# A fused decoder layer: attention values with the values stationary and the output transposed

## What is computed

```python
hn = rms_norm(x, norm_mix_g[l])
q_a, k_a, v_a, q_m, k_m, v_m, o_m, i_m, f_m = jnp.split(hn @ w_in[l], SPLIT_POINTS, axis=-1)
att = swa_sink_attention(q_a, k_a, v_a, ...)      # 8 heads of 64, 2 key/value heads, window 128, T5 bias, sink
h_m = mlstm_chunkwise(...)                        # 4 heads, normalised, gated
x = x + jnp.concatenate([att, h_m], axis=-1) @ w_out[l]
x = x + hier_moe(rms_norm(x, norm_ffn_g[l]), ...) # 16 experts, top 2 of one group of 4
...
# in the attention
p = jnp.exp(logits - m)
probs = p / (jnp.sum(p, axis=-1, keepdims=True) + jnp.exp(sink_l - m))
out = jnp.einsum('bnkgqs,bnskd->bnqkgd', probs, vb)
```

## Time and profile before

| | |
|---|---|
| median of 3 runs | 928.12 us (925.28 to 929.41) |
| the profiled execution | 928.41 us |
| its span, first to last instruction | 926.6 us |
| mean granted TensorE clock | 0.97 |
| TensorE busy | 868.4 us |
| VectorE busy | 616.1 us |
| ScalarE busy | 563.1 us |
| GpSimd busy | 250.0 us |

### The profile page before, as it was taken

The page is one execution under the profiler, slowest core; times in us unless marked ns, Lnnn a source line. Parts: engine busy times, 40 slices in busy tenths (PEclk is TensorE's granted clock), DMA queues, the critical chain, the costliest instruction groups (busy, mean ns, idle before and its releaser), DMA issues. The chain is left out here.

```text
span 926.6 us, 18029 instructions
## 1 busy us (share of the span) xinstructions
PE 868.4 (94%) x5329; PEld 697.2 (75%) x5330; DVE 616.1 (66%) x1257; ACT 563.1 (61%) x1004; POOL 250.0 (27%) x395
## 2 busy tenths in 40 slices
PE   5899999999999999999973899999999999999994
PEld 4679888898989887788862776776777788677873
DVE  3667666666566677643678766773769599775992
ACT  3473746556473857222241766783879799787991
POOL 4102021010101010000023243553354544445442
PEclk9989999999999998999995899999999999999997
DMA  9810000101010142344473877786698999779963
GB/s 329 250 27 24 24 23 23 45 0 45 0 45 23 47 182 69 137 157 138 159 273 119 316 264 228 257 306 157 228 350 318 322 392 392 269 277 337 393 254 68
DMA packets 57646, 168.41 MB, mean 182 GB/s; under 512 B 12584, under 2 KB 14928, under 8 KB 57616
## 3 DMA queue, kind: packets, MB, share of 16 engines
q1 hardware_dynamic: 50384, 143.13, 41.7%
q0 software_dynamic: 7232, 24.92, 10.4%
HBM read 143.49 MB, written 24.54 MB: 181 GB/s over the span
## 5 line engine op out<-in xcount | busy, mean ns | idle before, releaser
L1034 PE MATMUL bank_j<-w_high,rows_high 128*128 128x512 f32 x512 | 207.6, 405 | 8.0 <-DVE w_low L1637 5.5
L1036 PE MATMUL bank_j<-w_high,rows_low 128*128 128x512 f32 x512 | 201.8, 394 | 0.0
L1035 PE MATMUL bank_j<-w_low,rows_high 128*128 128x512 f32 x512 | 201.7, 394 | 0.0
L597 POOL TENSOR_TENSOR tick<-mhalf 1x1 f32<-1x1 f32 x176 | 89.4, 514 | 200.6 <-DVE lg L2064 73.7
L1034 PEld LDWEIGHTS bank_j<-w_high,rows_high 128*128 128x128 f32 x512 | 97.4, 190 | 39.8 <-issue 12.9
L1952 DVE TENSOR_TENSOR w_low<-w_res,w_high 128x1024 fp32r<-128x1024 f32 x96 | 114.2, 1217 | 7.1 <-ACT w_high L695 7.1
L1036 PEld LDWEIGHTS bank_j<-w_high,rows_low 128*128 128x128 f32 x512 | 97.3, 190 | 21.2
L1035 PEld LDWEIGHTS bank_j<-w_low,rows_high 128*128 128x128 f32 x512 | 97.6, 191 | 18.3
L695 ACT ACTIVATE w_high<-w_res 128x1024 fp32r<-128x1024 f32 x96 | 97.5, 1050 | 0.2 <-PE bank_j L1036 0.2
L1139 PE MATMUL bank_j<-hnT,w_res 128*128 128x128 f32 x512 | 60.3, 276 | 0.0
L543 POOL TENSOR_TENSOR rqk<-ssqk,eps_hd 128x10 f32<-128x10 f32 x8 | 5.8, 728 | 201.1 <-DVE ssqk L1833 201.1
(11 more groups left out here) (367 smaller groups left out, 1832.9 us busy)
## 6 DMA issues: line engine op xcount, KB each, us to landing
w_res<-in_w_gate_dram SPq DMA_DIRECT2D x48, 512.0 KB, 7.4
w_res<-in_w_up_dram SPq DMA_DIRECT2D x48, 512.0 KB, 7.2
bias<-in_w_down_dram SPq DMA_DIRECT2D x32, 512.0 KB, 7.5
slot_b<-in_w_gate_dram SPq DMA_DIRECT2D x16, 512.0 KB, 10.5
PT<-in_w_up_dram SPq DMA_DIRECT2D x16, 512.0 KB, 11.6
gmix<-in_w_down_dram SPq DMA_DIRECT2D x16, 512.0 KB, 6.5
h<-in_w_down_dram SPq DMA_DIRECT2D x16, 512.0 KB, 8.3
hn<-in_x_dram SPq DMA_DIRECT2D x8, 512.0 KB, 3.4
```

The source lines that it names most:

```text
L597: pool.tensor_tensor(tick[:, len(ticks):len(ticks) + 1], mhalf[0:1, 0:1], mhalf[0:1, 0:1], ALU.mult)
L1034: pe.matmul(out_, ah, bh, start=start, stop=False)
L1035: pe.matmul(out_, ah, bl, start=False, stop=False)
L1036: return pe.matmul(out_, al, bh, start=False, stop=stop)
```

## The change

`values` now keeps the values stationary, 64 columns of one key/value head at a time, and streams the transposed probabilities of two heads (256 columns). Its output is transposed: head columns by queries, the key/value head 0 in partitions 0 to 63 and head 1 in 64 to 127 of O0. The reciprocal sums must then be scaled per column. `prob_scales` (VectorE) spreads `arc` over 512 columns of `lg`, `sums_T` (TensorE) transposes them in four blocks into T0, `head_copy` (ScalarE) copies O0 into `mix`, and `attention` (VectorE) multiplies this in place with T0. The first 512 columns of a stored row tile are thus already transposed: `mix_T` transposes only the other half, and `mix_high` and `mix_low` read the first half from `hn` in SBUF. The rows of `w_out` are loaded in the matching order, and `load_mix` has stricter waits, since `hn` is read until `mix_low`. What the diff leaves out are the same calls in `last_tile` and its TensorE order, semaphore names, and one wait on a constant.

```diff
@@ -154,6 +154,7 @@
         rqk = sb("rqk", [P, KVH + HEADS])
         lg = sb("lg", [P, G, 2 * P])
         pr = lg
+        scales = lg[:, :, :].rearrange("p a b -> p (a b)")[:, 0:AW]
         PT = sb("PT", [P, G, 2, P])
         junk = PT[:, :, :, :].rearrange("p a b c -> p (a b c)")
         amx = sb("amx", [P, HEADS])
...
@@ -431,13 +432,18 @@
             def rows_of(dram, t):
                 return dram[t * P:t * P + P, :] if isinstance(t, int) else dram[bass.ds(t * P, P), :]
 
+            heads_out = w_out[0, 0:AW, :].rearrange("(g c d) n -> g c d n", g=KVH, c=G)
+
             def load_out(i):
-                sp.dma_start(slot_out[i], w_out[0, i * P:(i + 1) * P, :]).then_inc(ld_piece[i], 16)
+                if i < G:
+                    sp.dma_start(slot_out[i], heads_out[:, i, :, :]).then_inc(ld_piece[i], 16)
+                else:
+                    sp.dma_start(slot_out[i], w_out[0, i * P:(i + 1) * P, :]).then_inc(ld_piece[i], 16)
 
             def load_mix(t):
-                sp.wait_ge(st_mix, 16 * t + 16)
+                sp.wait_ge(st_mix, 16 * (t + 1 if isinstance(t, int) else TILES))
                 if not (isinstance(t, int) and t == 0):
-                    sp.wait_ge(pe_mixT, t)
+                    sp.wait_ge(dve_mixT, 2 * t)
                 sp.dma_start(hn[:, :], rows_of(mix_rows, t)).then_inc(ld_mix, 16)
 
             def body(t, u, main, nxt, ahead):
@@ -715,8 +721,8 @@
             def mix_high(t, u):
 
                 act.wait_ge(pe_mixT, t + 1)
-                for b in range(2):
-                    cp(MX[u][0][:, 4 * b:4 * b + 4, :].rearrange("p a b -> p (a b)"), TB[b][:, :]).then_inc(act_mixT, 1)
+                for b, src in enumerate((hn[:, 0:AW], T1[:, :])):
+                    cp(MX[u][0][:, 4 * b:4 * b + 4, :].rearrange("p a b -> p (a b)"), src).then_inc(act_mixT, 1)
 
             def route_exp(count, n):
 
@@ -753,6 +759,11 @@
                 for h in range(MH):
                     ins = act.activation(dmat[:, h, :], darg[:, h, :], ACT.Exp, bias=gT[:, h:h + 1])
                 ins.then_inc(act_D, 1)
+
+            def head_copy(t):
+                act.wait_ge(pe_o, t + 1)
+                wait(act, st_mix, 16 * t)
+                cp(mix[:, 0:AW], O0[:, :]).then_inc(act_att, 1)
 
             def state_squares(t, ssx_done):
                 act.wait_ge(dve_den, t + 1)
...
@@ -852,6 +864,7 @@
                         for i in range(8, PIECES):
                             in_high(i)
                 if main:
+                    head_copy(t)
                     state_squares(t, t + 2)
                 if into_last:
                     for i in range(2, 4):
@@ -1052,7 +1065,9 @@
 
             def mix_T(t):
                 pe.wait_ge(ld_mix, 16 * (t + 1))
-                transposes(hn, pe_mixT)
+                for i in range(4):
+                    ins = pe.transpose(T1[:, i * P:(i + 1) * P], hn[:, AW + i * P:AW + (i + 1) * P], ident[:, :])
+                ins.then_inc(pe_mixT, 1)
 
             def project_out(t, u, half):
 
@@ -1093,6 +1108,7 @@
                 v = 1 - u
                 if nxt:
                     pe.wait_ge(dve_hn, t + 2)
+                    wait(pe, dve_att, t)
                     transposes(hn, pe_hnT)
                 if main and not nxt:
                     mix_T(0)
@@ -1123,14 +1139,18 @@
                             ins = pe.transpose(TB[j // 2][:, c:c + P], pr[:, j, w * P:(w + 1) * P], ident[:, :])
                     ins.then_inc(done, 1)
 
-                def values(r, done):
-                    for j in range(G):
-                        h, g = round_head(r, j), j // RH
-                        for w, slot in ((0, v), (1, u)):
-                            ins = pe.matmul(O0[:, h * HD:(h + 1) * HD], PT[:, j, w, :],
-                                            vw[:, slot, g * HD:(g + 1) * HD], start=(w == 0), stop=(w == 1))
-                    if done is not None:
-                        ins.then_inc(done, 1)
+                def values(r):
+                    for w, slot in ((0, v), (1, u)):
+                        for g in range(KVH):
+                            pe.matmul(O0[g * HD:(g + 1) * HD, r * RH * P:(r + 1) * RH * P], vw[:, slot, g * HD:(g + 1) * HD],
+                                      PT[:, g * RH:(g + 1) * RH, w, :], start=(w == 0), stop=(w == 1),
+                                      skip_group_check=True)
+
+                def sums_T():
+                    pe.wait_ge(dve_arc, t + 1)
+                    for c in range(G):
+                        ins = pe.transpose(T0[:, c * P:(c + 1) * P], scales[:, c * P:(c + 1) * P], ident[:, :])
+                    ins.then_inc(pe_o, 1)
 
                 def conv_channels(cs):
 
...
@@ -1258,7 +1279,8 @@
                 if main:
                     pe.wait_ge(act_pT1, t + 1)
                     pe.wait_ge(dve_pT1, t + 1)
-                    values(1, pe_o)
+                    values(1)
+                    sums_T()
                     state_values()
                     pe.wait_ge(dve_kw, t + 1)
                     pe.wait_ge(dve_gT, t + 1)
@@ -1624,9 +1646,9 @@
 
             def mix_low(t, u):
 
-                for b in range(2):
+                for b, src in enumerate((hn[:, 0:AW], T1[:, :])):
                     dve.wait_ge(act_mixT, 2 * t + b + 1)
-                    dve.tensor_tensor(MX[u][1][:, 4 * b:4 * b + 4, :].rearrange("p a b -> p (a b)"), TB[b][:, :],
+                    dve.tensor_tensor(MX[u][1][:, 4 * b:4 * b + 4, :].rearrange("p a b -> p (a b)"), src,
                                       MX[u][0][:, 4 * b:4 * b + 4, :].bitcast(F32).rearrange("p a b -> p (a b)"),
                                       ALU.subtract).then_inc(dve_mixT, 1)
 
@@ -1717,17 +1739,22 @@
                         float(DQK) ** -0.5, dmat[:, b::2, :], ALU.mult, ALU.mult)
                 ins.then_inc(dve_sd, 1)
 
-            def attention(t):
-
-                dve.wait_ge(pe_o, t + 1)
+            def prob_scales(t):
+
                 dve.wait_ge(act_p1, t + 1)
+                wait(dve, pe_o, t)
                 chain(dve.tensor_tensor(arc[:, :], asum[:, :], aes[:, :], ALU.add))
                 chain(dve.reciprocal(arc[:, :], arc[:, :]))
-                wait(dve, st_mix, 16 * t)
-                dve.tensor_tensor(mix[:, 0:AW].rearrange("p (h d) -> p h d", h=HEADS),
-                                  O0[:, :].rearrange("p (h d) -> p h d", h=HEADS),
-                                  arc[:, :].unsqueeze(2).to_broadcast([P, HEADS, HD]), ALU.mult)\
-                    .then_inc(dve_att, 1)
+                dve.wait_ge(pe_pT1, t + 1)
+                dve.tensor_copy(scales.rearrange("p (c g d) -> p c g d", c=G, g=KVH),
+                                arc[:, :].rearrange("p (g c) -> p c g", g=KVH).unsqueeze(3)
+                                .to_broadcast([P, G, KVH, HD])).then_inc(dve_arc, 1)
+
+            def attention(t):
+
+                dve.wait_ge(pe_o, t + 1)
+                dve.wait_ge(act_att, t + 1)
+                dve.tensor_tensor(mix[:, 0:AW], mix[:, 0:AW], T0[:, :], ALU.mult).then_inc(dve_att, 1)
 
             def state_scales(t):
 
...
@@ -1850,6 +1877,7 @@
                                       ALU.mult).then_inc(dve_qkn, 1)
                 if main:
                     pT_copy(t, pe_pT1, dve_pT1)
+                    prob_scales(t)
                     state_weights(t)
                     if into_last:
                         out_low(0)
```

More of the change, by code:

```diff
@@ L242, in hymba_layer_program @@
         (pool_const, pe_brow, dve_brow, pe_bias, dve_bias) = sems("pool_const pe_brow dve_brow pe_bias dve_bias")
-        (pe_qkT, pe_hnT, pe_s0, pe_s1, pe_kvg, pe_g, pe_pT0, pe_pT1, pe_q, pe_pv0, pe_o, pe_cin, pe_st,
+        (pe_qkT, pe_hnT, pe_s0, pe_s1, pe_kvg, pe_g, pe_pT0, pe_pT1, pe_q, dve_arc, pe_o, pe_cin, pe_st,
          pe_vm, pe_h, pe_u, pe_om, pe_mixT, pe_y0, pe_y1, pe_h2T, pe_r) = sems(
-            "pe_qkT pe_hnT pe_s0 pe_s1 pe_kvg pe_g pe_pT0 pe_pT1 pe_q pe_pv0 pe_o pe_cin pe_st "
+            "pe_qkT pe_hnT pe_s0 pe_s1 pe_kvg pe_g pe_pT0 pe_pT1 pe_q dve_arc pe_o pe_cin pe_st "
             "pe_vm pe_h pe_u pe_om pe_mixT pe_y0 pe_y1 pe_h2T pe_r")
@@ L257, in hymba_layer_program @@
         (pool_wr, pe_rp, act_rp) = sems("pool_router_pad pe_router_parts act_router_parts")
-        (pool_rx, pool_rqk, pool_rhm, pool_rh, dve_const, dve_den) = sems("pool_rx pool_rqk pool_rhm pool_rh dve_const dve_den")
+        (pool_rx, pool_rqk, pool_rhm, pool_rh, act_att, dve_den) = sems("pool_rx pool_rqk pool_rhm pool_rh act_att dve_den")
         (dve_chain, act_chain, pool_chain) = sems("dve_chain act_chain pool_chain")
@@ L1195, in body @@
                     pe.wait_ge(dve_att, t)
-                    values(0, pe_pv0)
+                    values(0)
                     first_out([4])
@@ L1718, in state_weights @@
                 ins.then_inc(dve_sd, 1)
+            def prob_scales(t):
+                dve.wait_ge(act_p1, t + 1)
```

(20 more changed lines are left out.)

## The result

| | before | after |
|---|---|---|
| median | 928.24 us (925.28 to 929.41, 4 runs) | 947.75 us (946.17 to 948.83, 4 runs) |
| profiled span | 926.6 us | 945.9 us |
| mean granted clock | 0.970 | 0.958 |

The ratio is 1.021, 95% interval [1.0191, 1.0228]: the change costs 19.5 us, where 6 us of gain were forecast. The time is outside the range.

A forecast was written before the change was run, and what follows sets the result against it. TensorE, busy for 94% of the span, was taken as the bound. Tiles 0 to 5 -5.1, seam and tile 7 -1.1, projection 0: -6.2 us against the profiled 928.41, so 922 us, range 918 to 927.5.

The forecast's parts named there:

- the seam from tile 6 to tile 7: VectorE leads here; ScalarE's new copy behind the split of w_out piece 1 starts the squares 0.9 us later: +0.9 us.
- a load that costs: A store or load costing over several tiles; grouped with rival 1 under slower, together 0.07.
- copy of the scales: New VectorE 128x512 copy in each mixing tile, taken as 0.42 us; 0.69 without double rate.
- tiles 0 to 5: Ordinary mixing tiles: state values start earlier, 0.85 us gained each, 6 x -0.85 = -5.1 us.
- wait ahead of tile 7: TensorE's wait before tile 7, 1.3 us before, was to grow to about 3.5 us.
- tile 7 to the first h2_T: Last mixing tile, first round at 1.2 GHz: rounds and saved transposes gain 1.8 to 2.0 us, taken as -2.0.
- rival 1: Value rounds in every tile: column halves don't overlap, +1.2 us a tile, +9 in all, about 937 us; chance 6%.
- the 1.5 us of the prediction: Into the projection: the load of mixed rows, held by the last tile's store, is issued 1.5 us later.
- Rival 2: Before tile 7: longer idle brings the low clock again or for longer, costing 3.1 to 3.5 us: 925.5; chance 20%.
- Rival 3: Low-clock stretch around tile 7 goes away or falls where TensorE has slack: -3.3, 919 us; chance 10%.
- Rival 4: Mixing tiles: VectorE's scales hold TensorE before sums_T; tile gain only 0.5 us, 924.5 us; chance 12%.

The follow-up runs named there:

- e1: Changed kernel with each permuted w_out piece loaded by two transfers of 64 rows instead of one: 925.95 us, ratio 0.9969.
- e2: Kernel before with only the first four w_out pieces loaded from a source of 2 row blocks: 967.89 us, ratio 1.043, routing differs.
- e3: Kernel before with the first four w_out pieces loaded from 4 blocks of 32 rows: 956.88 us, ratio 1.0309, routing differs.
- e4: Kernel before with the first four w_out pieces loaded from 16 blocks of 8 rows: 904.36 us, ratio 0.975, routing differs.
- e13: Changed kernel with even heads on output partitions 0 to 63, odd on 64 to 127, w_out pieces plain, values pair by pair: 923.34 us, ratio 0.9951.
- e12: e13 plus ScalarE's squares moved ahead of the split of w_out piece 1 in tile 6: 919.58 us, ratio 0.9913.
- e5: e1 with ScalarE's copy of the values put ahead of the split of w_out piece 1 in tile 6: 923.34 us, ratio 0.995.
- e6: e1 with ScalarE's copy of the values and squares both ahead of the split of w_out piece 1 in tile 6: 923.1 us, ratio 0.9947.
- e9: e13 without the pair order of values, so part of the sums is left out and routing differs: 936.07 us, ratio 1.0091.
- e10: e9 plus ScalarE's squares ahead of the split of w_out piece 1; part of the sums left out: 933.12 us, ratio 1.0055.
- e7: Kernel before with only ScalarE's squares moved ahead of the split of w_out piece 1 in tile 6: 927.17 us, ratio 0.999.

## Why the prediction was wrong

**The step that failed** is the seam from tile 6 to tile 7, at the words "the DMA is issued at 332.89 [...], which is now some 0.65 earlier: 336.1". They take the landing of piece 1 from the kernel before and shift it, and never ask what the new source pattern does to the transfer; the text counts the other parts of the change one by one, and this line of the diff not at all. Piece 1 was taken 339.51 - 326.87 = 12.64 us after the issue, where the prediction kept the old 336.77 - 332.89 = 3.88, and pieces 2 and 3, for which ScalarE did not wait before, came some 11 us apart behind it. From tile 6's scores to tile 7's it is 370.66 - 305.78 = 64.88 us where it was 350.72 - 311.22 = 39.50: +25.4 stands in place of the step's +0.9. None of the rivals held it; "a load that costs" stood in the 7% for slower without a mechanism or a price. Shown: e1 takes the loss away, e2 makes it in the kernel before, and e3 and e4 scale it by the number of blocks.

**The rest of the sum**, by the kernels that load whole pieces or halves:

| term | forecast | measured |
|---|---|---|
| a round of values | 1.06 us | 1.01 (1.03 with 128 columns) |
| copy of the scales | 0.42 us | 0.43 |
| tiles 0 to 5 (scores 0 to scores 6) | 6 x -0.85 = -5.1 | -4.55 (after), -4.58 (e1), -4.40 (e13) |
| seam (start of scores 6 to start of scores 7) | +0.9 | +0.80 (e13), +1.60 (e1), -1.24 (e12) |
| wait ahead of tile 7 | 3.5 us | 3.3 (e13) |
| tile 7 to the first h2_T | -2.0 | -0.99 (e13), -0.74 (e1), -2.98 (e12) |
| first tile of the projection | +0.1 | -0.30 (e13: 13.74 us, before 14.04) |
| later tiles of the projection | 0 | 0.00: 13.71 us each, in before and e1 |

The scales, in VectorE's list of the changed kernel, with the state weights right behind them:

```profile
161.34 0.43 DVE L1749 COPY lg<-arc 128x512 f32<-128x512 f32 x1
161.68 0.75 DVE L1737 SCALAR_TENSOR_TENSOR darg<-bank_s,darg 128x256 f32<-128x256 f32 x2
```

The halves overlap, so rival 1 is out; the loop's gain is a tenth smaller than forecast. The load of the mixed rows is issued 2.03 us ahead of the first `h2_T` in e13, where it was 3.61: the 1.5 us of the prediction, and they cost nothing. Tile 7 gave half of its forecast. Rival 2 named a cause, the longer wait and the clock. Its form came in e1: the slow clock comes twice there, 6.8 us around the scores and 3.5 between 360 and 370 us, and the time is higher. In e13 it comes once, has the old length (6.8 us) and moves from the values of round 0 to the scores, where it covers matmuls that the change does not shorten. With that round at full speed TensorE is then ahead of the exponentials, and waits for them in front of tile 7's second transposes, in e13 and in e12, where the kernel before has no such wait. The line of e12, from 345 us on:

```profile
PE bank_t L1132 <- ACT aes L734: 1.1, 1, 1.1
```

The prediction has the wait at this place only for an ordinary tile, where it is nothing. Rival 3 came in e12, where the slow stretch goes away. Rival 4 is out: the copy takes 0.43 us and no wait stands at the sums. With whole pieces, the measured terms of e13 add up to -4.4 + 0.8 - 1.0 - 0.3 = -4.9 us, its loop starts 0.39 us later than before, and its ratio, 0.9951 of 928.24, says -4.5. So the rest of the sum has the right mechanism and is too good by some 1.7 of its 6.2 us, nearly all of it in the loop (0.7) and in tile 7 (1.0).

Where the loss of the change stands, against e13: the seam 43.90 - 19.30 = +24.6 us, the medians 947.75 - 923.34 = +24.4.

## What to carry to other kernels

When an edit changes the access pattern of a load, even one made once, cost it as a new transfer: look at its slowest dimension, because a source in 2 blocks used 2 of 16 DMA engines, and a piece came every 11 us where a plain one needs some 1.3 (an estimate: 524,288 bytes at 400 GB/s, between the 369 and 416 above). Then find who waits for it, and what is queued behind that wait. A layout in which the weights stay in their order (even and odd heads on the two halves of the array) gives the same gain with no new load. And a longer wait can bring TensorE's slow clock onto work that ran fast: shortening the wait from 3.3 to 1.2 us, e13 to e12, was worth 3.8 us.

## What the runs showed of the hardware that was not expected

- A transfer from 2 blocks of rows went over 2 DMA engines (share 0.13, 53 GB/s), from 4 over 4 (0.25, 102 GB/s), from 16 over all, but at 246 GB/s (1.04).
- Issuing is held up as well. Of three such transfers the first two took 0.51 and 0.55 us of SyncE's queue and the third 8.43, 9.58 us in all, and the next three, plain, took 12.51 us, where six plain ones take 3.00 us in e12:

```profile
328.58 3.00 SPq L436 DMA_DIRECT2D w_res<-in_w_out_dram  x6
336.18 0.35 SPq L468 DMA_DIRECT2D mix_rows<-h  x1
```

  The store of the mixed rows, a plain one, was thus issued at 351.0 in place of 336.2 us. Why plain transfers are held by the ones ahead of them was not tried.
- Two transfers of 64 rows use all 16 engines, yet the load ran at 259 GB/s, where whole pieces ran at 380 in e12 and at 412 in e1 itself, behind the halves (338 to 340 us). The reason stays open, as for the 246 GB/s of the 16 blocks.
- The slow clock came in e1, e5, e6, e9 and e13, all with a wait of 2.9 us or more ahead of tile 7, and within it or just behind, in e1, e6 and e9 a second time between 360 and 370 us; in e12 and e10, with 1.2 us, not at all; in the kernel before and e7, with 1.3 and 1.1 us, it came later, at 362 us. A wait's length alone does not tell it.
